# Router by token halves, token groups written out, and an earlier first gate in a two-layer expert-choice encoder

## What is computed

```python
def expert_choice_ffn(h, router_w, wg, wu, wd):   # h = rms_norm(x, norm2_w)
    aff = jax.nn.softmax((h @ router_w).astype(jnp.float32), axis=-1)
    gate, idx = lax.top_k(jnp.swapaxes(aff, 1, 2), C)          # C = 32
    xs = jnp.take_along_axis(h, flat_idx[..., None], axis=1).reshape(B, N_EXPERTS, C, D)
    a = jnp.einsum('becd,edf->becf', xs, wg)                   # D = 1024, F = 1408
    u = jnp.einsum('becd,edf->becf', xs, wu)
    o = jnp.einsum('becf,efd->becd', jax.nn.silu(a) * u, wd) * gate[..., None]
    return jax.vmap(lambda oi, ii: jnp.zeros((S, D), h.dtype).at[ii].add(oi))(o, flat_idx)
```

## Time and profile before

| | us |
|---|---|
| median of three runs | 2001.66 |
| lowest and highest | 2000.48, 2001.76 |
| the profiled execution, whole | 2003.29 |
| its span, first to last instruction | 2001.5 |
| TensorE busy | 1563.8 |
| VectorE busy | 560.0 |
| ScalarE busy | 286.2 |
| layer 0: first load after the router issued, last down weights landed | 404.3, 998.3 |
| layer 1: the same | 1398.1, 1985.2 |

### The profile page before, as it was taken

How to read it: one execution, slowest core, us unless ns; L and a number is a source line. 1 busy time by engine, 2 the same in 40 slices (tenths; PEclk the granted TensorE clock), 3 DMA queues, 4 the chain that set the end, 5 groups by cost and what they waited for, 6 DMA issues and landing times.

```text
span 2001.5 us, 22268 instructions
## 1 busy us (share of the span) xinstructions
PE 1563.8 (78%) x9588; PEld 879.5 (44%) x9588; DVE 560.0 (28%) x1073; ACT 286.2 (14%) x600; POOL 45.7 (2%) x24
## 2 busy tenths in 40 slices
PE   8999999876576665676799999998765765666767
PEld 5687688432232232222256877884222221322322
DVE  3654771211111111111136547712111111111211
ACT  3233210110000000000132332101100100000010
POOL 0300000000000000000002000000000000000000
PEclk9999999898788887888899999998886878877888
DMA  7522055699999999999966221545999999999998
GB/s 294 227 89 84 1 230 206 250 393 425 432 428 433 435 427 434 434 430 411 423 218 231 85 84 40 237 181 244 437 431 426 432 436 428 430 434 430 431 419 341
DMA packets 26135, 644.57 MB, mean 322 GB/s; under 512 B 2864, under 2 KB 3888, under 8 KB 6320
## 3 DMA queue, kind: packets, MB, share of 16 engines
q1 hardware_dynamic: 24976, 638.47, 75.7%
q10 hardware_dynamic: 1056, 4.53, 0.8%
HBM read 641.94 MB, written 1.05 MB: 321 GB/s over the span
## 4 chain that ended last, share of the span: by engine, by line
PE 51%; DMA 45%; issue 1%; DVE 1%; ACT 1%; DVEq 0%; SPq 0%; ACTq 0%
DMA region<-w_down_dram 41%; PE ps L872 10%; PE ps L487 7%; PE ps L554 6%; PE ps L694 6%; DMA region<-w_down_last_dram 3%; PE ps L767 3%; PE ps L824 2%; PE ps L515 2%; PE ps L677 1%; PE ps L630 1%; PE ps L577 1%; PE ps L532 1%; PE ps L666 1%; PE ps L814 1%
## 5 line engine op out<-in xcount | busy, mean ns | idle before, releaser
L824 PE MATMUL ps<-ring,region 128*32 128x384 f32 (+1 forms) x2944 | 292.1, 531 | 184.9 <-DMA ring<-w_gbu_dram 184.9
L872 PE MATMUL ps<-region,late 128*32 128x512 f32 x1320 | 205.2, 742 | 124.1 <-DMA region<-w_down_dram 121.3
L824 PEld LDWEIGHTS ps<-ring,region 128*32 128x32 f32 x2944 | 120.1, 123 | 351.7 <-DMA ring<-w_gbu_dram 202.3
L487 PE MATMUL ps<-xnT,ring 128*128 128x256 f32 x768 | 178.3, 380 | 4.3 <-DVE region L1148 2.6
L1486 DVE TENSOR_TENSOR region<-region,ps 128x256 f32<-128x256 f32 x32 | 13.5, 421 | 549.7 <-PE ps L824 549.7
L872 PEld LDWEIGHTS ps<-region,late 128*32 128x32 f32 x1320 | 50.9, 133 | 257.5 <-issue 156.5
L487 PEld LDWEIGHTS ps<-xnT,ring 128*128 128x128 f32 x768 | 140.7, 190 | 23.8 <-DVE region L1148 4.4
L890 PE MATMUL ps<-region 128*128 128x512 f32 x256 | 124.3, 617 | 27.7 <-ACT region L1128 21.6
L554 PE MATMUL ps<-xnT,ring 128*128 128x256 f32 x512 | 115.8, 381 | 0.0
L1500 DVE TENSOR_TENSOR x<-x,ps 128x512 f32<-128x512 f32 x128 | 88.0, 688 | 83.0 <-PE ps L890 83.0
L1497 DVE COPY region<-ps 128x512 f32<-128x512 f32 x32 | 22.1, 692 | 314.8 <-PE ps L872 314.2
(11 more groups left out here) (204 smaller groups left out, 1482.1 us busy)
## 6 DMA issues: line engine op xcount, KB each, us to landing
region<-w_down_dram SPq DMA_DIRECT2D x28, 5632.0 KB, 32.9
ring<-w_gbu_dram SPq DMA_DIRECT2D x30, 4928.0 KB, 32.7
region<-w_ga_dram SPq DMA_DIRECT2D x14, 6336.0 KB, 36.8
ring<-w_ga_dram SPq DMA_DIRECT2D x12, 6336.0 KB, 34.8
ring<-units_dram SPq DMA_DIRECT2D x28, 2048.0 KB, 8.4
region<-units_dram SPq DMA_DIRECT2D x6, 2048.0 KB, 12.1
ring<-w_ga_dram SPq DMA_DIRECT2D x2, 4288.0 KB, 13.6
region<-w_down_dram SPq DMA_DIRECT2D x4, 2048.0 KB, 10.7
```

The costliest lines, as they stand in the source:

```text
L487: m = mm(bank(b % 2, S), unit8(n)[:, i, j * P:(j + 1) * P], xnT[:, i], start=i == 0, stop=i == DB - 1)
L824: m = mm(bank(b, QW[j], rows=CAP, row0=CAP * j), xs[:, i, q * CAP:(q + 1) * CAP], w[i][:, j * FT:j * FT + QW[j]], start=i == 0, stop=i == ...
L872: m = mm(bank(c, rows=CAP, row0=CAP * j), hT[:, b * P + CAP * j:b * P + CAP * (j + 1)], wd[:, CT * b + j, c * 512:(c + 1) * 512], start=b ...
```

## The change

The change is made in four places.

1. The router goes by token halves. `w_out` is multiplied for token half 0 (both column halves), then for half 1. The transposes and logits of half 0 are put between the k-steps of the last product; squares, roots, maxima, exponentials and affinities are taken for each half by itself. The normed x of half 0 is made before the exponentials.
2. WARM is 5 instead of 4, two more such products stand before the affinities' transposes, and none of them waits for the normed x.
3. Picked rows go in four pairs of blocks instead of two fours, with a scaling each. In expert 0 only the first two pairs precede the gate; the other two stand between gate rows 3 and 4. The place of expert 0's A comes free in four parts: row 0, rows 1 to 3, rows 4 and 5, the rest. TensorE's groups are written out instead of looped; VectorE's stay in the loop.
4. A of the last expert is loaded in two parts: rows 0 and 1 before the down load of expert 14, the rest after it.

```diff
-WARM = 4
+WARM = 5
@@ sync
-                        sp.wait_ge(s["wout_psum"], L * 4 + 2 * (n - 14))
+                        sp.wait_ge(s["wout_psum"], L * 4 + (3 if n == 15 else 4))
...
-                sp.wait_ge(s["lgT_psum"], L + 1)
+                sp.wait_ge(s["lgT_psum"], (L + 1) * SB)
                 load_gate_a_second(12 * 1024 + SPARE, REGION - 3072)
                 for e in range(1, E):
                     if e == 1:
-                        sp.wait_ge(s["gate_h"], L * E + 1)
-                        load_gate_a_third(slice(0, 4 * FF), s["wga_third_in"])
+                        for k, (r0, r1) in enumerate(((0, 1), (1, 4), (4, 6))):
+                            sp.wait_ge(s["gate_rows"], 3 * L + k + 1)
+                            load_gate_a_third(slice(r0 * FF, r1 * FF), s["wga_third_in"])
                         sp.wait_ge(s["gate_a"], L * E + 1)
-                        load_gate_a_third(slice(4 * FF, A_COLS), wga_in[0])
+                        load_gate_a_third(slice(6 * FF, A_COLS), wga_in[0])
...
                     elif e == E - 1:
-                        sp.wait_ge(s["gate_a"], L * E + e - 1)
-                        load_gate_a(e)
+                        load_gate_a_last(slice(2 * FF, A_COLS), wga_in[1])
                     sp.wait_ge(s["up_done"], L * E + e + FREE)
                     (load_gate_b_up if e < E - 1 else load_gate_b_up_last)(e)
+                    if e == E - 2:
+                        sp.wait_ge(s["gate_a"], L * E + e)
+                        load_gate_a_last(slice(0, 2 * FF), s["wga_last_in"])
@@ tensor
+                w_out(0, 0, 0, DB)
+                w_out(0, 1, 0, DB)
+                w_out(1, 0, 0, DB)
+                x_transposed(0, 0)
+                x_transposed(0, 1)
+                w_out(1, 1, 0, 3)
                 pe.wait_ge(s["fvec_in"], 16 * (L + 1))
...
+                logits_by_k(0)
+                x_transposed(1, 0)
+                w_out(1, 1, 3, 6)
+                logits(0)
+                w_out(1, 1, 6, DB)
+                x_transposed(1, 1)
+                logits_by_k(1)
+                logits(1)
+
+                def warm(count):
+                    for _ in range(count):
+                        mm(bank(0, S), ident, x3[:, 0, 0:S], start=True, stop=True)
+
+                warm(2)
+                pe.wait_ge(s["aff_dve"], (L + 1) * SB)
...
-                pe.wait_ge(s["xn2_act"], L + 1)
-                for _ in range(WARM):
-                    mm(bank(0, S), ident, xn2[:, 0, 0:S], start=True, stop=True)
+                warm(WARM)
...
+                    def picked_rows(b):
+                        if b >= 2:
+                            pe.wait_ge(s["xs_dve"], 4 * (L * NG + g) + b - 1 + FREE)
+                        for i in (2 * b, 2 * b + 1):
+                            for t in range(SB):
+                                m = mm(bank(b % 2, P, (i % 2) * P), xn2[:, t, i * P:(i + 1) * P], pick[:, t],
+                                       start=t == 0, stop=t == SB - 1)
+                        m.then_inc(s["xs_psum"], 1)
+
+                    picked_rows(0)
+                    picked_rows(1)
+                    if g:
+                        picked_rows(2)
+                        picked_rows(3)
...
                         for i in range(DB):
-                            if q == 0 and i % 4 == 0:
-                                pe.wait_ge(s["xs_dve"], 2 * (L * NG + g) + i // 4 + 1 + FREE)
+                            if e == 0 and i == 4:
+                                picked_rows(2)
+                                picked_rows(3)
+                            if q == 0 and i % 2 == 0:
+                                pe.wait_ge(s["xs_dve"], 4 * (L * NG + g) + i // 2 + 1 + FREE)
                             m = product(2, wg[q % 2], i)
-                            if i == 3:
-                                m.then_inc(s["gate_h"], 1)
+                            if e == 0 and i in (0, 3, 5):
+                                m.then_inc(s["gate_rows"], 1)
...
-                with pe.Fori(0, NG - 1) as g:
-                    group(g, False)
-                group(NG - 1, True)
+                for g in range(NG):
+                    group(g, g == NG - 1)
@@ scalar
+                squares(0, 0)
                 act.wait_ge(s["fvec_in"], 16 * (L + 1))
...
+                mean_of_first(0)
+                squares(0, 1)
+                root(0)
+                scaled_copies(0, 1)
+                scaled_copies(0, 3)
+                normed(0)
+                squares(1, 0)
+                mean_of_first(1)
+                scaled_copies(1, 1)
+                squares(1, 1)
+                root(1)
+                scaled_copies(1, 3)
+
                 for t in range(SB):
...
+                    act.wait_ge(s["lmax_dve"], L * SB + t + 1)
+                    af(aff[:, t], bank(5 + t, E, t * E), ACT.Exp, bias=lmax[:, t:t + 1],
+                       scale=n2[:, t:t + 1], accum_out=lmax[:, 2 + t:3 + t]).then_inc(s["lexp_act"], 1)
+                normed(1)
@@ vector
+                x_mid(0)
+                x_mid(1)
+                x_mid(2)
+                scaled_copies(0, 0)
+                scaled_copies(0, 2)
+                inverse_norm(0)
+                logits_by_k(0)
+                scaled_copies(1, 0)
+                largest(0)
+                x_mid(3)
+                scaled_copies(1, 2)
+                inverse_norm(1)
+                logits_by_k(1)
+                largest(1)
+                affinities(0)
+                affinities(1)
```

More of the change, by code:

```diff
@@ L1415, in _, with x_mid @@
                     tt(mT[:, i], gm[:, 0:S], gm[:, S:2 * S], ALU.add).then_inc(s["merged_dve"], 1)
-                for k in range(4):
-                    c, t = k // 2, k % 2
+                def x_mid(k):
+                    t, c = k // 2, k % 2
                     dve.wait_ge(s["wout_psum"], L * 4 + k + 1)
```

178 lines of the change are left out of this document (84 added, 94 removed).

## The result

The changed kernel takes 1988.53 us (median of four runs, 1987.34 to 1989.56) against 2001.71 us for the kernel before on the same chip (four runs, 2000.48 to 2003.5). The ratio is 0.9937, with a 95% interval of 0.9925 to 0.9949. That is a gain of 12.6 us by the ratio, where 9.1 us were forecast; the time forecast, 1992.6 us, is 4.1 us too long, and 1988.53 lies in the range. Later runs of the kernel before, 13 to 19 in each comparison, have medians of 2001.1 to 2001.3, so its profiled execution (2003.3 us) was on the long side. Single executions scatter by 2 us or more, and I compare profiles by differences inside them.

What follows compares the result with a forecast made beforehand. The prediction took the DMA stream of expert weights, and when it may start, to bound the kernel. Its terms, 3.5 + 3.6 + 0 + 1.6 + 0.4 = 9.1 us, took 2001.66 to 1992.6 us, range 1987 to 1998.5.

Steps and rivals of the forecast that it cites:

- The stream's start bounds the kernel: Weight stream from expert 2's gate load: every us it starts earlier is a us of the result, once per layer.
- Size of the earlier start: Start of the weight stream behind the router: earlier by 3.5 us in layer 0 and 3.6 us in layer 1.
- the start that counts: Second issue of expert 2's gate weights less 1.7 us of row 0's bytes: 400.8 and 1394.5.
- the moment at which the clock rises: TensorE in layer 0's first gate rows: granted clock taken to rise near 400.5, the same moment as before.
- All later parts in time: Expert 2's later gate parts and the next loads: issued before their turn in the queue, nothing falls behind.
- The four parts: Expert 2's gate load: row 0 as its own 704 KB part starts the stream 1.7 us before the second issue.
- P by zero: Router by halves: start of the picked-row products unmoved, 1.4 us added against 1.2 saved; bounds 1.5 earlier to 2.5 later.
- Groups written out: TensorE's group loop, two turns per layer: removing the jumps gains 4 x 0.4 = 1.6 us, from 0 to 6.
- Last expert's gate: Two gate rows ahead of expert 14's down load cover a queue gap: 0.4 us gained for both layers.
- slower: Rival: clock stays at 1.2 GHz through expert 0, so the next gate/up load passes its turn; 2009.6 us, chance 0.05.
- The sum: Whole kernel: 3.5 + 3.6 + 0 + 1.6 + 0.4 = 9.1 us gained, giving 1992.6 us.
- clock up at P: Rival: extra warm-ups keep the full clock at the picked-row products; gains 7.0 and 5.2 us, 1987.5 us, chance 0.14.

Runs made afterwards that it cites:

- run 1: Kernel before with only TensorE's token groups written out instead of looped; 1999.55 us, ratio 0.9991.
- run 3: Changed kernel with the router, its warm-ups and the waits on them as before; 1990.48 us, ratio 0.9948.
- run 8: Changed kernel with the last expert's A loaded whole after expert 14's down load, as before; 1989.33 us, ratio 0.9942.
- Run 7: Changed kernel with expert 2's A loaded in two parts (rows 0 to 3, then the rest) instead of four; 1989.57 us, ratio 0.9947.
- run 10: Changed kernel with TensorE's first three groups looped, one more warm-up in the maxima rounds and two before the picked rows; 1983.59 us, ratio 0.9912.
- run 2: Kernel before with only the new router and its warm-ups, loop and old gate order kept; 1992.11 us, ratio 0.9951.
- run 5: Kernel before with 96 already-met waits (48 TensorE instructions) ahead of each layer's first products; 2000.82 us, ratio 0.9998.
- run 9: Kernel before with 84 already-met waits (42 instructions) where TensorE waits for the exponentials; 1996.14 us, ratio 0.9973.
- run 6: Changed kernel with TensorE's groups 0 to 2 looped again, all groups in the new first group's order; 1986.03 us, ratio 0.9925.
- run 11: Changed kernel with TensorE's first three groups looped, WARM 4 and no two products before the affinities' transposes; 1986.12 us, ratio 0.9922.
- run 4: Changed kernel with 256 waits per expert added to GpSimd's program, to fetch more instructions; 1997.72 us, ratio 0.9978.

## Why the prediction was right, and where it was not

**The stream's start bounds the kernel: right.** The steps from run 1 to run 3 show it best, since their packets are equal: W to D1 falls by 6.2 and 2.8 us, together 9.06, and the median by 9.1 us. That the two agree to a tenth is luck: the 9.1 us hold the last expert's gate too, and in run 3's profiled execution the clock was full at P in layer 0. The two spans differ by 11.5 us.

**Size of the earlier start: right in layer 1, under in layer 0.** The second issue less 1.7 us was to be the start that counts, P + 5.7 and P + 4.6. It was P + 4.65 and P + 4.54 (399.83 - 1.7 - 393.48, 1386.43 - 1.7 - 1380.19). The step that failed in layer 0 is the moment at which the clock rises: I took 400.5, P + 5.4, by the window of before; in the window 395 to 400 of the kernel after the granted clock is already 0.83, and the first four gate rows run in 2.78 us, the full clock's rate, from 396.99 on. The clock came up with the products' end, not at the same moment as before.

**All later parts in time: right.** The third and fourth issue are 3.4 and 5.3 us behind the second (forecast 3.1 to 4.9 and two more), the gate/up load is issued at 409.69 and the down load at 416.97, both before their turn, and 400 to 405 has no hole.

**Landings gain less than the start.** Relative to W the start that counts comes 6.0 us earlier in layer 0 (52.69 - 46.71) and 4.35 in layer 1 (50.99 - 46.64); D1 gains 5.5 and 2.8. The missing 0.5 and 1.5 us were in no term. Most of them can be scatter of a single execution: in run 8, with nothing changed ahead of D1, it gains 6.0 and 4.1.

**The four parts: the term was at its upper end.** Run 7 gives 1.7 to 3.5 us by landings and 1.0 by the median (within the scatter of four runs), where 3.4 were taken. The Trainium skill, DMA: Bandwidth & Descriptors, section Rules for kernel authors, wants at least 1 MiB per DMA; at half rate for the 704 KB the parts would have brought nothing, and the landings show a gain in both layers. The runs don't separate the part's rate from the wait between the parts.

**P by zero: wrong, 1.5 and 0.7 us early.** Three things, from the timelines. The new order brings the affinities' transposes to W + 34.96 instead of W + 35.23 (386.38 less 351.42; the earlier trace rows, 386.84 less 351.61), 0.3 us in both layers. That is the part which the prediction's sum covers: the last product ends 1.4 us later behind W, as forecast (381.15 less 351.42 is 29.73, give 28.34), and from there to the transposes it takes 5.2 us, where 5.7 were added up. Then I had said that the warm-up products could end with the maxima, as they do now, and cost nothing. The kernel before shows that they didn't end with them; its VectorE, then TensorE:

```profile
391.14 0.40 DVE L1451 MATCH_REPLACE8 region<-late,region 16x256 f32<-16x256 f32 x1
```

```profile
388.36 3.75 PE L793 MATMUL ps<-xnT,consts 128*128 128x256 f32 x8 [0.94 <-ACT xnT L1112]
```

The rounds end at 391.54 and the warm-ups at 392.11: they start late, because they wait for the normed x. After, ten of them start at 386.72 and end at 390.61, ahead of the rounds' end, and the turning of the picks follows VectorE at 391.10 after 0.49 us of idle time. Relative to the affinities' transposes it comes 0.5 us earlier in layer 0 and 0.2 in layer 1. The third part, from the turning to P, is 0.7 and 0.2 us. 0.2 us of it in both layers belongs to the written-out groups and not to the router: the idle time ahead of P is 1.30 or 1.31 us in every looped kernel (but run 10, which fills it), and 1.11 or 1.12 in every written-out one, run 1 included. The other 0.5 us in layer 0 is that the ranks run at the full clock (0.38 and 0.37 us, before 0.61 and 0.59). **The row for the second point stood in the trace of before; I had read the end of the warm-ups without laying it beside the end of the maxima.** Run 3 puts what the router has of this at 2.0 us of the time.

**Groups written out: the sum right by luck, the step behind it wrong.** The forecast put 0.4 us on each of four jumps. Run 1 gave 1.6 us, but run 2 keeps all four jumps and loses nothing at them, and runs 5 and 9 make a jump free by adding instructions in front of it. What costs is the fetching, and whether a replayed loop is fetched depends on where in the program it begins. The body of the loop is 1592 instructions of TensorE, 6.2 packets of 256 (52 packets are the program of 13,427 instructions once; 0.85 MB / 52 = 16 KB a packet). It is fetched anew where it begins at 13.70 and 39.70 packets into the program (kernel before) and not where it begins at 13.82 to 13.91 and 39.95 to 40.14 (runs 2, 5, 6, 9, 10, 11). These places are counted in the programs; where the bound lies between 13.70 and 13.82, or whether layer 1's 39.70 alone decides its own layer, no run shows.

The Trainium skill, Runtime: NRT & Kernel Launch, section Instruction fetch mechanics, says that a taken branch forces a fetch unless its target is in the current two-page window, that the cost of crossing a block is mostly hidden, and that kernels prefer full unrolling where possible. It also gives TensorE a buffer of 2048 instructions, in which the loop's 1592 would fit, and has no word on why its place would matter. Runs 2 and 6 speak against the three as rules for this kernel: in run 2 a jump back over six packets fetches nothing, landings with packets between them are up to 1.5 us late in a stream that is DMA-bound, and the looped kernel of run 6 is 2.5 us faster than the unrolled one. That the stall at a jump, where one happens, is hidden by the stream was forecast and held.

**Last expert's gate:** 0.4 forecast, 0.8 measured, no more than the scatter. (A slip in the rival "slower", of no weight: its own places, P + 28.4 against P + 24.2 and P + 23.2, give 4.2 and 5.2 us, where it has 4.5 and 5.4.)

**The sum.** Forecast 3.5 + 3.6 + 0 + 1.6 + 0.4 = 9.1. Measured in the medians: 8.3 for the first two (9.1 less 0.8), 2.0, 1.6 and 0.8, together 12.7. The misses of 1.2, 2.0 and 0.4 all have the same sign; the one term that was too large, the four parts, is inside the 8.3. The rival "clock up at P" gave 1987.5, closer to the result than the forecast, but it isn't what happened: at P the clock was at half in both layers. Nothing of "slower" was seen: the clock was full from 397 on.

**What stays open.** Layer 0's tail, from D13 to layer 1's W, is 2.1 us shorter after (412.23 against 414.31). It is also short in runs 2, 7, 8, 9 and 11 (412.2 to 412.8), and not in runs 1, 3, 4, 6 and 10 (413.0 to 414.9). Most of the short ones have the new router, but run 9 has the old one, and runs 4, 6 and 10 have the new. It may be no more than scatter, and no run isolates it. Nor is it settled why a packet delays one landing and not another: in the stretch above the kernel after has 12 packets, and of its landings two are over 1 us late.

## What to carry to other kernels

Where a kernel streams weights at the DMA engines' full rate, look at the intervals between landings, not at the engines: here the departures from the even interval belonged to something that goes through the same engines, TensorE's own instructions. Count the instruction packets of the page before deciding to unroll a loop; here a loop that is replayed without fetching was better than a written-out one, and a few instructions ahead of it decided it. Warm-up products are to fill the gap right before the work, and are never to stand behind a wait of their own that can end later than what they cover.

## What the runs showed of the hardware

- **An instruction packet costs the stream more than its share of the bytes.** 16 KB of TensorE's instructions are 0.04 us at 433 GB/s over 16 engines, but landings with packets between them are up to 1.1 to 1.5 us late (41.09, 41.14, 41.53 against 39.98), and 32 packets of 8 KB for GpSimd made 9.2 us. The earlier trace rows show what one packet takes of one engine: 0.8% of 16 engines over 42 us, for 5 packets, is 1.1 us each, where data go at 0.6 us for the same 16 KB (99.8% of 16 engines over 330 us for 3547 packets of 141.81 MB). The reading that fits is that a packet holds one of the 16 DMA engines for about that long, and that a landing waits for the engine furthest behind; no run tried it apart. Many packets are not seen in the landings at all: the 24 that the kernel after has more than run 6 cost 2.5 us together.
- **A loop of 6.2 packets can be replayed without any fetch**, for two turns of 160 us, and is fetched anew in the kernel before, where it begins 0.12 to 0.21 packets earlier in layer 0 and 0.25 to 0.44 in layer 1. Without a fetch nothing of TensorE's time is lost at the jump (1.37 us idle ahead of the picked rows); with one it is 5.77 and 3.59 us of "issue".
- **Waits that are met cost TensorE 0.11 us an instruction of two waits** (run 5: 5.24 us for 48, while nothing else held the first products).
- **The granted clock at P is not fixed by one gap.** In the kernels with sixteen products ahead of the gate these took 2.02 to 3.78 us. With 0.35 us idle ahead of P it was 2.02 in both layers (2.4 GHz); with 1.1 to 1.3 us it was mostly 3.4 to 3.8 (1.2 GHz), but 2.05 in layer 0 of run 3 with 1.12 us idle, where the warm-ups of the old router end later, and between the two in four others (2.52 to 3.07).
